# Blocks of B and C one trip ahead in a hybrid decoder block: the first beside the index scores, the last trip filled with the attention output

## The reference

```
def hybrid_layer(x, ...):
    h = rms_norm(x, g_norm1)
    proj = h @ w_in
    c_q, c_kv, k_idx, w_idx, z, xbc, dt_raw, gate_a, gate_b = jnp.split(proj, IN_OFFSETS, axis=-1)
    cq = rms_norm(c_q, g_cq)
    ckv = rms_norm(c_kv, g_ckv)
    q = rms_norm((cq @ w_uq).reshape(b, s, ATTN_HEADS, ATTN_HEAD_DIM), g_qn)
    kv = (ckv @ w_ukv).reshape(b, s, ATTN_HEADS, 2 * ATTN_HEAD_DIM)
    k = rms_norm(kv[..., :ATTN_HEAD_DIM], g_kn)
    v = kv[..., ATTN_HEAD_DIM:]
    q_idx = (cq @ w_iq).reshape(b, s, IDX_HEADS, IDX_DIM)
    attn = sparse_attention(q, k, v, q_idx, k_idx, w_idx * IDX_HEADS ** -0.5)
    y_a = attn.reshape(b, s, ATTN_HEADS * ATTN_HEAD_DIM) @ w_o_attn
    y_b = mamba2_mixer(z, xbc, dt_raw, conv_w, conv_b, dt_bias, a_log, d_skip, g_ssm) @ w_o_ssm
    mixed = jax.nn.sigmoid(gate_a) * y_a + jax.nn.sigmoid(gate_b) * y_b
    x = x + mixed @ w_out
    x = x + peer_ffn(rms_norm(x, g_norm2), w_peer_q, peer_keys, peer_u, peer_v)
    return x
```

## Time and profile before

| | |
|---|---|
| median of three runs | 2637.36 us (2636.16 to 2637.39) |
| the profiled execution | 2636.65 us, of which the span from the first to the last instruction is 2635.0 us |
| mean granted clock of TensorE | 0.817 of full speed |
| busy over the span | PE 64%, DVE 62%, ACT 33%, POOL 24% |
| index scores (first matmul to last score) | 82.2 to 105.8 us |
| top-k and mask | 107.9 to 125.7 us |
| attention loop | 107.5 to 288.9 us, from the second trip on 43.56 us each |
| attention output | 288.9 to 381.4 us |

### The profile page before, as it was taken

The page is one execution under the profiler, slowest core; times in us unless marked ns, Lnnn a source line. Parts: engine busy times, 40 slices in busy tenths (PEclk is TensorE's granted clock), DMA queues, the critical chain, the costliest instruction groups (busy, mean ns, idle before and its releaser), DMA issues.

```text
span 2635.0 us, 29465 instructions
## 1 busy us (share of the span) xinstructions
PE 1685.6 (64%) x9753; PEld 1260.1 (48%) x9753; DVE 1622.4 (62%) x2480; ACT 867.0 (33%) x1738; POOL 638.4 (24%) x617
## 2 busy tenths in 40 slices
PE   7899999999999999999962222322232232223225
PEld 6798878888888888978960000000000000000001
DVE  5887637766767766775686766666654444444441
ACT  4466445545545445545442022201221101111000
POOL 1000000100001001040034644443443343333332
PEclk9799999999999999999986666666666566666666
DMA  5244556665665655556589999999999999999998
GB/s 181 81 152 141 168 159 196 199 190 167 194 189 174 192 186 181 174 189 219 197 339 419 420 420 420 420 420 420 420 420 420 420 420 421 420 420 420 420 420 325
DMA packets 211420, 774.26 MB, mean 294 GB/s; under 512 B 18968, under 2 KB 54160, under 8 KB 144016
## 3 DMA queue, kind: packets, MB, share of 16 engines
q0 software_dynamic: 75584, 549.49, 50.7%
q1 hardware_dynamic: 135264, 223.61, 27.4%
q10 hardware_dynamic: 496, 0.23, 0.0%
HBM read 771.09 MB, written 2.16 MB: 293 GB/s over the span
## 4 chain that ended last, share of the span: by engine, by line
PE 45%; DMA 37%; DVE 9%; issue 5%; POOL 2%; ACT 1%; DVEq 0%; POOLq 0%; ACTq 0%; SPq 0%
DMA u_slots<-in_peer_u_dram,eid 32%; PE accA L1624 5%; PE accA L1626 5%; PE accA L1625 5%; DVE u_slots L1481 4%; PE accB L1624 4%; PE accB L1626 4%; PE accB L1625 4%; DMA v_slots<-in_peer_v_dram,v_eid 4%; PE accB L1618 2%; PE accB L1616 2%; PE accB L1617 2%; PE small L1634 1%; DVE w_lo L1062 1%; PE pair_d L1616 1%
## 5 line engine op out<-in xcount | busy, mean ns | idle before, releaser
L1481 DVE CUSTOM_DVE_ANT_0 u_slots<-u_slots,h 128x2048 f32<-128x2048 f32 x256 | 586.3, 2292 | 519.7 <-DMA u_slots<-in_peer_u_dram,eid 494.3
L1062 DVE TENSOR_TENSOR w_lo<-w_raw,w_hi 128x1024 fp32r<-128x1024 f32 (+1 forms) x420 | 523.3, 1256 | 291.7 <-ACT w_hi L724 290.4
L724 ACT ACTIVATE w_hi<-w_raw 128x1024 fp32r<-128x1024 f32 (+1 forms) x420 | 442.1, 1057 | 422.7 <-PE accB L1626 139.6
L660 POOL DMA_INDIRECT u_slots<-in_peer_u_dram,eid x256 | 262.0, 1023 | 780.5 <-DVE dots L1481 523.4
L1951 PE MATMUL accA<-v_slots,weight 128*32 128x512 f32 x512 | 113.7, 1038 | 482.5 <-DMA v_slots<-in_peer_v_dram,v_eid 482.5
L1951 PE MATMUL small<-v_slots,weight 128*32 128x512 f32 x496 | 111.1, 1045 | 413.4 <-DMA v_slots<-in_peer_v_dram,v_eid 413.4
L684 POOL DMA_INDIRECT v_slots<-in_peer_v_dram,v_eid x252 | 271.3, 1076 | 110.8 <-issue 82.3
L1951 PEld LDWEIGHTS accA<-v_slots,weight 128*32 128x32 f32 x512 | 21.9, 158 | 550.7 <-issue 550.7
L1951 PEld LDWEIGHTS small<-v_slots,weight 128*32 128x32 f32 x496 | 21.2, 158 | 481.5 <-issue 481.5
L1035 ACT ACTIVATE gelu_s<-dots 32x4 f32<-32x4 f32 x256 | 52.9, 207 | 589.0 <-DVE dots L1481 586.1
L1616 PE MATMUL accB<-act_hi,w_hi 128*128 128x256 f32 x512 | 145.1, 283 | 2.1 <-ACT ya L890 1.1
(11 more groups left out here) (370 smaller groups left out, 3829.6 us busy)
## 6 DMA issues: line engine op xcount, KB each, us to landing
w_raw<-in_w_in_dram SPq DMA_DIRECT2D x168, 512.0 KB, 3.7
w_raw<-in_w_in_dram SPq DMA_DIRECT2D x128, 256.0 KB, 3.1
w_raw<-in_w_o_ssm_dram SPq DMA_DIRECT2D x64, 512.0 KB, 3.8
w_raw<-in_w_o_attn_dram SPq DMA_DIRECT2D x32, 512.0 KB, 4.5
w_raw<-in_w_out_dram SPq DMA_DIRECT2D x32, 512.0 KB, 4.4
w_raw<-in_w_peer_q_dram SPq DMA_DIRECT2D x32, 512.0 KB, 4.6
cum_row<-cum_dram POOLq DMA_DIRECT2D x8, 1024.0 KB, 7.5
w_raw<-in_w_uq_dram SPq DMA_DIRECT2D x8, 512.0 KB, 5.4
```

Of the source, the lines that this page charges most:

```text
L660: pool.indirect_dma_start(u_slots[:, n % U_RING, :], None, peer_u[0], bass.IndirectOffsetOnAxis(ap=eid[:, u, k:k + 1], axis=0)).then_inc(u ...
L724: act.activation(w_hi[:, slot, :, 0:w], w_raw[:, slot, :, 0:w], ACT.Copy).then_inc(hi_split, 1)
L1062: dve.tensor_tensor(w_lo[:, slot, :, 0:w], w_raw[:, slot, :, 0:w], w_hi[:, slot, :, 0:w].bitcast(F32), ALU.subtract).then_inc(lo_split, 1)
L1481: dve.tensor_tensor_reduce(slot, slot, h2[:, u // PH, :], 1.0, 0.0, ALU.mult, ALU.add, dots[:, u % 2, k:k + 1]).then_inc(u_free, 1)
```

## The change

It renumbers the pieces and moves work:

- **First block of B and C.** Its eight pieces get numbers between `w_iq` and the loop (`n_bc0`). TensorE multiplies five of them behind index heads 2, 5, 8, 11 and 14 (`BC0_AT`) and three behind head 15, ahead of `cum`. ScalarE's splits stand at the same places, and its bias ahead of the loop.
- **GpSimd splits.** The `w_lo` of these eight pieces and of the three after them are written by GpSimd; VectorE's five ticks in the index scores and the top-k go.
- **VectorE ahead of the loop:** behind `keep` it waits for GpSimd's splits, splits two pieces and adds the taps of the first block.
- **The loop** has three trips, each with the *next* block of B and C.
- **The last trip** stands apart. In the places of `bc(0)` to `bc(4)` and `bc(7)` it multiplies the first six pieces of `w_o_attn` (into `pair_d`); in those of `bc(5)` and `bc(6)` nothing; the last two pieces of that block follow the trip. It has no taps at its end. The other three blocks go to A, B, A, with a wait for ScalarE's copies only before the last.

```
+        BC0_AT = (2, 5, 8, 11, 14)
+        POOL_SPLITS = KP + 3
...
+            pool.wait_ge(lo_split, n_bc0)
+            for n in range(n_bc0, n_bc0 + POOL_SPLITS):
+                slot = n % RING
+                pool.wait_ge(hi_split, n + 1)
+                pool.tensor_tensor(w_lo[:, slot, :, :], w_raw[:, slot, :, :], w_hi[:, slot, :, :].bitcast(F32),
+                                   ALU.subtract).then_inc(lo_split, 1)
+            with pool.Fori(0, J - 1) as j:
...
+                if h in BC0_AT:
+                    tick(At(n_bc0 + BC0_AT.index(h)))
...
+            for k in range(len(BC0_AT), KP):
+                tick(At(n_bc0 + k))
+            done(act, At(n_attn - 1))
+            bias_bc(0, 1)
             for k in range(2):
                 tick(At(n_attn + k))
...
-                if h in (11, 12, 13):
-                    tick(At(n_idx + h - 10))
...
-                tick(At(n_attn + t))
...
-            with dve.Fori(0, J) as j:
+            dve.wait_ge(lo_split, n_bc0 + POOL_SPLITS)
+            for k in range(2):
+                tick(At(n_attn + k))
+            conv_taps(bc_t, pair_d, 4)
+
+            def trip(j, last=False):
...
-                tick(at(10))
-                tick(at(11))
+                if not last:
+                    tick(at(10))
+                    tick(at(11))
...
-                conv_taps(bc_t, pair_d, j * 4 + 4, j * 4)
-
-                tick(at(J_P))
-                tick(at(J_P + 1))
-                steps.leave(J)
-
-            for k in range(2, 4 * KP):
+                if not last:
+                    conv_taps(bc_t, pair_d, j * 4 + 8, j * 4 + 4)
+
+                    tick(at(J_P))
+                    tick(at(J_P + 1))
+                    steps.leave(J - 1)
+
+            with dve.Fori(0, J - 1) as j:
+                trip(j)
+            trip(J - 1, True)
+            for k in range(KP - 2, 4 * KP):
                 tick(At(n_ya + k))
...
+                if h in BC0_AT:
+                    bc0(BC0_AT.index(h))
+
+            for k in range(len(BC0_AT), KP):
+                bc0(k)
             pe.wait_ge(small_free_act, IDXH)
             pe.wait_ge(da_lo, 1)
...
+                    if not last:
+                        pieces(at(4), range(first, first + n), BANK, pair_d, True)
+                    else:
+                        for k in range(first, first + n):
+                            if k in YA_AT:
+                                ya_first(YA_AT.index(k))
...
+            YA_AT = (0, 1, 2, 3, 4, 7)
+
+            def ya_first(k):
+                piece(At(n_ya + k), BANK, pair_d, attn_hi, attn_lo, 2 * k, k == 0, k == KP - 1, False)
...
+            for k in (6, 7):
+
+                pe.wait_ge(acc_free_dve, af_dve_y - 7 + k)
+                ya_first(k)
+            for b, o in ((1, A), (2, B), (3, A)):
+                pe.wait_ge(acc_free_act, af_act_y + (2 if b == 3 else 0))
+                for k in range(KP):
+                    piece(At(n_ya + b * KP + k), BANK, o, attn_hi, attn_lo, 2 * k, k == 0, k == KP - 1, False)
```

More of the change, by code:

```diff
@@ L109, in hybrid_block @@
     n_all = n_pq + 4 * KP
-    assert all(n % RING == 0 for n in (n_idx, n_attn, J_P, n_ya, n_ssm, G_P, n_wout, n_pq, n_all))
+    assert all(n % RING == 0 for n in (n_idx, n_bc0, n_attn, J_P, n_ya, n_ssm, G_P, n_wout, n_pq, n_all))
     IN2 = KVL + IDXD + IDXH + SH
@@ L828, in _, with trip @@
             q_gain, k_gain = columns[:, c_cqg + 6:c_cqg + 7], columns[:, c_cqg + 7:c_cqg + 8]
-            with act.Fori(0, J) as j:
+            def trip(j, last=False):
                 def at(k):
-                    return At(n_attn + k, j, J_P)
+                    return At(n_attn + (J - 1) * J_P + k) if last else At(n_attn + k, j, J_P)
                 def use(k):
@@ L874, in _ @@
                                    A[:, r, :], ACT.Copy).then_inc(turned_hi, 1)
[L875 to L880, removed]
-                tick(at(J_P))
-                tick(at(J_P + 1))
+                if not last:
+                    done(act, at(11))
+                    bias_bc(j * 4 + 4, j + 2)
+                    tick(at(J_P))
+                    tick(at(J_P + 1))
+            with act.Fori(0, J - 1) as j:
+                trip(j)
+            trip(J - 1, True)
             for k in range(4 * KP):
-                if k >= 2:
+                if k >= KP - 2:
                     tick(At(n_ya + k))
@@ L1687, in _, with bc0 @@
             pe.wait_ge(qi_split, 2)
+            def bc0(k):
+                pieces(At(n_bc0), range(k, k + 1), BANK, pair_d, True)
             for h in range(IDXH):
@@ L1708, in _, with trip @@
             pe.matmul(cum[:, 1, :], cum_rhs0[:, 0, :], da_split[:, 3, :], start=False, stop=True).then_inc(small_full, 1)
-            with pe.Fori(0, J) as j:
+            def trip(j, last=False):
                 def at(k):
-                    return At(n_attn + k, j, J_P)
+                    return At(n_attn + (J - 1) * J_P + k) if last else At(n_attn + k, j, J_P)
                 def act_free(n):
@@ L1721, in bc @@
                 def bc(first, n=1):
-                    pieces(at(4), range(first, first + n), BANK, pair_d, True)
+                    if not last:
+                        pieces(at(4), range(first, first + n), BANK, pair_d, True)
[3 more added lines that the diff above has]
+                                ya_first(YA_AT.index(k))
                 def turn_pair(src, k):
@@ L1796, in _ @@
                 weigh(1)
-            pe.wait_ge(small_free_dve, sf_dve_g)
[L1800 to L1806, removed]
+            YA_AT = (0, 1, 2, 3, 4, 7)
+            def ya_first(k):
+                piece(At(n_ya + k), BANK, pair_d, attn_hi, attn_lo, 2 * k, k == 0, k == KP - 1, False)
+            with pe.Fori(0, J - 1) as j:
+                trip(j)
+            trip(J - 1, True)
+            for k in (6, 7):
[5 more added lines that the diff above has]
+                    piece(At(n_ya + b * KP + k), BANK, o, attn_hi, attn_lo, 2 * k, k == 0, k == KP - 1, False)
+            pe.wait_ge(small_free_dve, sf_dve_g)
+            pe.wait_ge(acc_free_act, af_act_y + 1)
             for t in range(NT):
```

32 lines of the change are left out of this document (21 added, 11 removed).

## The result

| | before | the change |
|---|---|---|
| median | 2637.38 us (20 runs, 2633.41 to 2639.90) | 2641.05 us (20 runs, 2638.74 to 2644.90) |
| ratio | 1 | 1.0016, 95% interval 1.0010 to 1.0023 |
| profiled execution | 2636.65 us, span 2635.0 | 2638.95 us, span 2637.5 |
| mean granted clock | 0.817 | 0.815 |

What follows compares the result with a forecast made beforehand. VectorE's scoring was taken to bound the index scores, TensorE the trips and output blocks. Front +19.4 and tail -19.4 gave 0 against 2636.65 us; 0.7 for the median and half a microsecond for blocked starts made 2638, range 2631 to 2650.

Steps and rivals of the forecast that it cites:

- The gate: Before the top-k: running sums, queued on TensorE behind all eight pieces, end at 121.9 us; top-k starts 14.4 us later.
- Top-k, splits and taps: VectorE ahead of the loop: top-k with mask 15.45 us, two splits 2.3, taps 5.16, before `ss` at 145.3 us.
- The trips between: Loop trips two and three: keep their 43.56 us, with the same eight pieces in them.
- The front: First index head to running sums: first piece to about 89.7 us, four groups of 5.5, sums ending at 121.9.
- The lock: Rival, index scores: GpSimd's splits block VectorE's two-input scoring; groups of 6.5 us, +4, 2642 us; chance 0.12.
- The oscillating clock: Rival, index groups: clock falls between pieces, 8.0 us a group instead of 5.5, +10, 2648 us; chance 0.20.
- the term of the last trip: Last loop trip, two places without their piece: ends only 0.3 us earlier, near 288.6 instead of 288.88.
- The output: Attention output behind the last trip, six pieces already done: 19.1 us less.
- The four terms: First head to `ss` +19.4 us, `ss` to last trip 0, last trip -0.3, from there through the output -19.1.
- The shrinking trip: Rival, last trip: it shrinks by `bc(5)` and `bc(6)`, 5.8 us more; with a full-clock front 2630 us; chance 0.18.

Runs made afterwards that it cites:

- e1_late_copy: The change with VectorE's copy of the running sums moved from ahead of the top-k to behind the mask: 2633.93 us, ratio 0.9981.
- e2_dve_splits: The change with all eleven of GpSimd's splits given back to VectorE: 2641.66 us, ratio 1.0014.
- e6_three_late: The change with three pieces among the index heads, five behind the last, and VectorE's copy of the running sums behind the mask: 2633.67 us, ratio 0.9985.
- e3_dummy_fill: The change with twelve unused matmuls of 512 columns added in each of the last trip's two empty places: 2641.42 us, ratio 1.0012.
- e4_real_fill: The change with the attention output's pieces reordered, so the last trip's two empty places take two pieces of the third block: 2635.17 us, ratio 0.9988.
- e7_all: e6_three_late with the last trip filled by real pieces as in e4_real_fill: 2626.05 us, ratio 0.9958.
- e10_mixed_fill: e6_three_late with six splits on VectorE, GpSimd's last five after the top-k's first instruction, and the last trip filled: 2619.48 us, ratio 0.9937.

## Why the prediction held, and what it had wrong

**The gate held.** The running sums ended at 122.9 us against the 121.9 forecast, the top-k followed at 123.1, and e1_late_copy shows the cause: without that order 7 to 9 us come back. **Top-k, splits and taps** took 22.7 us, forecast 23.0. **The trips between** kept their length.

**The front was 1.2 us longer than forecast.** The first piece took 5.15 us instead of 4.5, as the clock came up near 89.5 and not at 88.8; the groups took 5.63 us instead of 5.5; the third head ended 0.3 later. Top-k to `ss` gave back 0.3.

**The lock cost nothing, for the reason given.** The scoring pairs beside a split took 2.9 to 3.0 us, the scores were done by 115.2 and then VectorE waited 7.70 us; e2_dve_splits changed nothing. Where the cover was taken away (e6_three_late) it cost 4.4 us, inside the 2 to 6 of the forecast. By the Trainium skill (SBUF — State Buffer, "SBUF: two separate sides") a VectorE instruction with two SBUF inputs contends for the lock with a GpSimd instruction that reads SBUF. The runs agree on both sides: 0.68 us became 2.89 with two inputs, and the top-k's rounds stayed at 0.29 and 0.41 beside five splits.

**The oscillating clock was not there**, neither in the change (1.00 from 90 to 112 us) nor, as a pattern of every group, elsewhere. With four heads in a row and GpSimd's splits beside them it fell once (0.63 from 100 to 104 us in e6_three_late); with the same four heads and VectorE's splits it stayed at 1.00.

**The step that failed is the term of the last trip:** "The trip so ends only 0.3 us earlier". Up to the weighted values it was right: they started 36.95 us into the trip instead of 37.49, with 4.96 us of waits ahead of them where "5 to 6 us" were forecast. What it left out is what those waits do to the clock. From there to the trip's end TensorE has the same count of work as before, and took 8.80 us instead of 6.07, at 0.50 for 6 us. -0.5 + 2.7 is the +2.2 measured, where -0.3 stood. The Trainium skill (TensorE: Matmul & The Clock Gate, "HAM oscillation — how this bites in real kernels") tells of such a fall when one long wait comes in every round; here three shorter ones, of at most 2.30 us, did it. I weighed that rule for the index groups, where TensorE never paused for more than 0.35 us, and not for the one place where I had forecast the pauses myself. It is no accident of one execution: in all seven profiled kernels with the two places empty the clock fell to 0.50 here and the trip took 44.6 to 46.0 us, 7.7 to 9.0 of them from the weighted values on; in the four with the places full (e3_dummy_fill, e4_real_fill, e7_all, e10_mixed_fill) the clock stayed at 1.00, and it took 43.2 to 43.3 us, 5.99 of them from there.

**The output** gave 19.3 us, forecast 19.1. The four terms together give +3.6, and the medians differ by 3.7; that the two agree so closely is partly luck, since the same last trip took from 44.6 to 46.0 us in single executions.

**The shrinking trip** (the rival of the other sign) was wrong in its mechanism: taking the pieces out frees no time. Putting other pieces in frees their time elsewhere, which is e4_real_fill's 6 to 8 us.

So the change is a move from one full place to another, as argued; its gain was lost to the order of a single 0.29 us copy on VectorE (7 to 9 us), to two empty places in the last trip (6 to 7 us; in the trace 2.4 by the clock), and to GpSimd's splits where the scores end (4.4 us in the trace, visible only once the first is mended).

## What to carry to other kernels

When work is moved on one engine, look for the smallest instruction elsewhere that waits for the end of that engine's queue: here a copy of 0.29 us held a top-k of 15.5 us, and moving it was worth more than where the large work stands. Where pieces are taken out of a tight sequence, count the pauses that they leave not only as time but for the clock of what follows, and fill them with work from behind. Give GpSimd elementwise work beside VectorE instructions like these max and match-replace, with one large SBUF input, not beside short ones with two.

## What was unexpected of the hardware

- A short VectorE instruction with two SBUF inputs pays a whole GpSimd operation: 0.28 us became 2.50 and 0.68 became 2.89, one behind the other, as GpSimd's next split began between them. GpSimd's own splits took 2.3 to 2.7 us.
- VectorE's max and match-replace beside the same splits took exactly their usual time.
- Three waits of TensorE of 1.69, 0.97 and 2.30 us within 6 us, with 1 us of small matmuls between, left the granted clock at 0.50 for the 6 us of dense work that followed; one of 8.53 us ahead of the fourth piece of the first trip did so too (0.50 from 134 to 144 us), but under VectorE's splits and taps, where it cost nothing.
- From the end of the attention output to the end of the span, single executions took 2253.2 us (the change) to 2258.8 (e3_dummy_fill) with the same code. Whether part of an earlier start is given back there, or it is scatter alone, stays open; it bounds what one profile can say of the whole.
